# State-space groups: clipped distances move from VectorE to ScalarE one slab sooner, convolution goes ahead of mask and norm, softplus in four parts

## The reference, cut to what matters

```python
z, xbc, dt_raw, u_pool, gate_logits = jnp.split(h @ w_in, IN_SPLITS, axis=-1)
xbc = silu(causal_depthwise_conv(xbc, conv_w, conv_b))      # 4 taps
xs, bmat, cmat = jnp.split(xbc, ...)
dt = softplus(dt_raw + dt_bias);  a_cont = -exp(a_log)
a_cs = cumsum(dt * a_cont)
M[l, s] = (cmat[l] . bmat[s]) * exp(a_cs[l] - a_cs[s])      # for s <= l, else 0
y = M @ (xs * dt) + d_skip * xs                             # per head
y = rmsnorm(y * silu(z)) per group;  y_ssd = y @ w_branch_ssd
```

## Time and profile before

| | us |
|---|---|
| median of three runs | 1355.06 |
| lowest, highest | 1347.4, 1355.24 |
| the profiled execution | 1352.02 |
| its span, first to last instruction | 1350.1 |
| its mean granted TensorE clock | 0.966 of full |

### The profile page before, as it was taken

The page is one execution under the profiler, slowest core; times in us unless marked ns, Lnnn a source line. Parts: engine busy times, 40 slices in busy tenths (PEclk is TensorE's granted clock), DMA queues, the critical chain, the costliest instruction groups (busy, mean ns, idle before and its releaser), DMA issues.

```text
span 1350.1 us, 27191 instructions
## 1 busy us (share of the span) xinstructions
PE 1271.1 (94%) x9944; PEld 1235.0 (91%) x9944; DVE 957.2 (71%) x1728; ACT 698.0 (52%) x1077; POOL 28.8 (2%) x58
## 2 busy tenths in 40 slices
PE   6878899999999999999999989999999998999997
PEld 6867899999999999999999879899899997999997
DVE  4574578888788886778888888787876555555554
ACT  4325465555545445455555566666665334544442
POOL 0000000000000000000000000000000000000000
PEclk9889899999999999999999979999999998899998
DMA  6421356666467555856665525445336453455540
GB/s 262 125 63 63 134 179 205 207 210 222 168 234 261 194 208 223 266 169 208 217 215 179 182 91 192 141 155 171 124 126 199 159 187 125 142 186 186 182 160 31
DMA packets 71007, 234.66 MB, mean 174 GB/s; under 512 B 7056, under 2 KB 15376, under 8 KB 70304
## 3 DMA queue, kind: packets, MB, share of 16 engines
q1 hardware_dynamic: 63280, 203.87, 45.2%
q0 software_dynamic: 7664, 29.92, 6.7%
HBM read 232.69 MB, written 1.08 MB: 173 GB/s over the span
## 4 chain that ended last, share of the span: by engine, by line
PE 48%; DVE 31%; issue 10%; ACT 9%; DVEq 1%; DMA 0%; ACTq 0%; SPq 0%; PEldq 0%
PE ps L182 14%; PE ps L184 13%; PE ps L183 13%; DVE w_lo L174 13%; DVE arena L827 3%; ACT w_hi L169 3%; DVE arena L821 2%; DVE arena L829 2%; ACT arena L771 2%; PE ps L213 2%; DVE arena L1527 1%; DVE b_lo L850 1%; DVE arena L357 1%; ACT arena L565 1%; PE ps L1267 1%
## 5 line engine op out<-in xcount | busy, mean ns | idle before, releaser
L182 PE MATMUL ps<-a_hi,w_hi 128*128 128x256 f32 x1912 | 561.3, 294 | 9.4 <-DVE a_lo L1136 5.3
L174 DVE TENSOR_TENSOR w_lo<-w_raw,w_hi 128x1024 fp32r<-128x1024 f32 x381 | 462.1, 1220 | 142.8 <-ACT w_hi L169 140.5
L183 PE MATMUL ps<-a_lo,w_hi 128*128 128x256 f32 x1912 | 549.3, 287 | 0.0
L184 PE MATMUL ps<-a_hi,w_lo 128*128 128x256 f32 x1912 | 548.8, 287 | 0.0
L182 PEld LDWEIGHTS ps<-a_hi,w_hi 128*128 128x128 f32 x1912 | 375.1, 196 | 21.8 <-issue 14.8
L169 ACT ACTIVATE w_hi<-w_raw 128x1024 fp32r<-128x1024 f32 x381 | 386.7, 1046 | 13.9 <-DMA w_raw<-stream 7.2
L183 PEld LDWEIGHTS ps<-a_lo,w_hi 128*128 128x128 f32 x1912 | 375.8, 197 | 0.6 <-issue 0.2
L184 PEld LDWEIGHTS ps<-a_hi,w_lo 128*128 128x128 f32 x1912 | 375.4, 196 | 0.0
L182 PE MATMUL ps<-b_hi,w_hi 128*128 128x256 f32 x928 | 265.4, 286 | 8.0 <-DVE b_lo L850 4.1
L183 PE MATMUL ps<-b_lo,w_hi 128*128 128x256 f32 x928 | 262.5, 283 | 0.0
L184 PE MATMUL ps<-b_hi,w_lo 128*128 128x256 f32 x928 | 262.5, 283 | 0.0
(11 more groups left out here) (248 smaller groups left out, 1190.1 us busy)
## 6 DMA issues: line engine op xcount, KB each, us to landing
w_raw<-stream SPq DMA_DIRECT2D x381, 512.0 KB, 4.1
arena<-ada POOLq DMA_DIRECT2D x48, 512.0 KB, 5.5
c_hi<-cum_rows POOLq DMA_DIRECT2D x4, 1024.0 KB, 5.7
con<-consts SPq DMA_DIRECT2D x1, 1440.0 KB, 13.0
arena<-x SPq DMA_DIRECT2D x1, 1024.0 KB, 5.1
out<-arena SPq DMA_DIRECT2D x2, 512.0 KB, 3.0
arena<-c_rows POOLq DMA_DIRECT2D x1, 512.0 KB, 7.0
par<-params SPq DMA_DIRECT2D x1, 319.0 KB, 5.5
```

Of the source, the lines that this page charges most:

```text
L174: dve.tensor_tensor(w_lo[:, s % RING], w_raw[:, s % RING], w_hi[:, s % RING].bitcast(F32), ALU.subtract).then_inc(w_lo_ready, 1)
L182: pe.matmul(o, wh, xh, start=start, stop=False, skip_group_check=shared)
L183: pe.matmul(o, wh, xl, start=False, stop=False, skip_group_check=shared)
L184: return pe.matmul(o, wl, xh, start=False, stop=stop, skip_group_check=shared)
```

## The change

- `gaps` goes from VectorE to ScalarE. It is there a relu of cum[s] - cum[l] (bias a column of `cum_tok`, scale -1), and the exp takes scale -1. `neg_cum` becomes `cum_tok`, without its sign.
- ScalarE does relus and exps of two heads in slots 7 to 10 (`decays`), where the exps stood in 8 to 11, between `split_hi` and `used`. `decays(0)` waits for the spread cumulative sums and in group 0 for `own_copied`, `decays(2)` for the b_lo of the group before.
- VectorE, slot 5: convolution first, then the mask. The norm of the group before moves from slot 5 to slot 6, its b_lo behind x times dt in slot 7. ScalarE's copy into b_hi moves behind `split_hi` and silu(5) in slot 6. In the gates the norm moves from m = 5 to m = 6 too.
- The softplus is cut into four parts, behind the convolutions of slots 0 to 3 of group 0; `own` goes from slab 4 to slab 5, the copies of its result from slot 5 to slot 6, behind `split_lo`.
- In the gates the spread goes from m = 3 to m = 4.

```diff
@@ TensorE
-                    if j == 4 and not g:
+                    if j == 5 and not g:
                         own()
@@ gates
-                if m == 3:
+                if m == 4:
                     tail_spread(GROUPS - 1, None)
@@ ScalarE
+                def gaps(k):
+                    if k >= 4:
+                        act.wait_ge(y_done, in_group(k - 3, 8, g, it))
+                    for b in range(NB):
+                        c = slice(0, SEQ) if b == 0 else slice(SEQ, SEEN)
+                        ...
+                        act.activation(seen[k % 4][:, c], cum_all[:, k, b * P:SEQ], ACT.Relu, bias=cum_tok[:, b, h],
+                                       scale=-1.0).then_inc(gap_ready, 1)
+                def exps(k):
+                    act.wait_ge(gap_ready, in_group(2 * k + 2, 16, g, it))
+                    act.activation(seen[k % 4], seen[k % 4], ACT.Exp, scale=-1.0).then_inc(exp_done, 1)
+                def decays(k):
+                    if k == 0:
+                        act.wait_ge(cum_landed, in_group(16, 16, g, it))
+                    if k == 0 and not g:
+                        act.wait_ge(own_copied, 1)
+                    if k == 2 and g:
+                        act.wait_ge(yssd_ready, in_group(1, 1, g - 1, it))
+                    gaps(k)
+                    gaps(k + 1)
+                    exps(k)
+                    exps(k + 1)
                 for j in range(GRP):
-                    if g:
+                    if g and j != 6:
                         tail(j, g - 1, it)
                     split_hi(act, S_GRP + GRP * g + j + 3, it, GRP)
-                    if j >= 8:
-                        exps(2 * (j - 8))
-                        exps(2 * (j - 8) + 1)
                     if j == 6:
                         silu(5)
+                    if g and j == 6:
+                        tail(j, g - 1, it)
+                    if 7 <= j < 11:
+                        decays(2 * (j - 7))
                     used(j)
@@ VectorE
-                if j == 5:
+                if j == 6:
                     dve.wait_ge(inv_s_ready, in_group(1, 1, g, it))
...
                 for j in range(GRP):
-                    if g:
+                    if g and j != 7:
                         tail(j, g - 1, it)
-                    elif j in (0, 1):
-                        (softplus_series, softplus_and_cum)[j]()
                     split_lo(dve, S_GRP + GRP * g + j + 3, it, GRP)
-                    if j == 5:
-                        (wait for cb_ready, mask)
                     if j < 6:
                         ... (three taps)
+                    if j < 4 and not g:
+                        softplus_part(j)
+                    if j == 5:
+                        (wait for cb_ready, mask)
-                    if j == 5 and not g:
+                    if j == 6 and not g:
                         dve.wait_ge(own_ready, 1)
                         (copies of own)
                     if j == 7:
                         (x times dt)
+                    if g and j == 7:
+                        tail(j, g - 1, it)
                     if j >= 8:
                         (products of decay and mask)
-                    if 7 <= j < 11:
-                        gaps(2 * (j - 7))
-                        gaps(2 * (j - 7) + 1)
```

More of the change, by code:

```diff
@@ L1159, in build @@
         dt_f = area(SEQ)
-        dt_tok, neg_cum = area(NB, SSD_HEADS), area(NB, SSD_HEADS)
+        dt_tok, cum_tok = area(NB, SSD_HEADS), area(NB, SSD_HEADS)
         root_s = area(NB)
@@ L1369, in silu @@
                     act.activation(cv[:, j], cv[:, j], ACT.Silu).then_inc(act_done, 1)
-                def exps(j):
-                    act.wait_ge(gap_ready, in_group(2 * j + 2, 16, g, it))
-                    act.activation(seen[j % 4], seen[j % 4], ACT.Exp).then_inc(exp_done, 1)
+                def gaps(k):
[3 more added lines that the diff above has]
+                        c = slice(0, SEQ) if b == 0 else slice(SEQ, SEEN)
+                        h = GROUP_HEADS * g + k
+                        h = slice(h, h + 1) if it is None else bass.ds(it * GROUP_HEADS + h, 1)
+                        act.activation(seen[k % 4][:, c], cum_all[:, k, b * P:SEQ], ACT.Relu, bias=cum_tok[:, b, h],
[14 more added lines that the diff above has]
+                    exps(k + 1)
                 for j in range(GRP):
-                    if g:
+                    if g and j != 6:
                         tail(j, g - 1, it)
                     split_hi(act, S_GRP + GRP * g + j + 3, it, GRP)
-                    if j >= 8:
-                        exps(2 * (j - 8))
-                        exps(2 * (j - 8) + 1)
                     if j == 6:
                         silu(5)
+                    if g and j == 6:
+                        tail(j, g - 1, it)
+                    if 7 <= j < 11:
+                        decays(2 * (j - 7))
                     used(j)
@@ L1444, in ssd_vec @@
             dve.scalar_tensor_tensor(out=dt_e[h], in0=dt_x[h], scalar=-1.0, in1=dt_x[h], op0=ALU.mult, op1=ALU.max).then_inc(dt_x_ready, 1)
[L1446 to L1463, removed]
+            def softplus_part(n):
+                if n == 0:
+                    dve.wait_ge(dt_e_ready, 1)
+                    step(dve.tensor_scalar(dt_z[h], dt_e[h], 2.0, None, ALU.add))
+                    step(dve.reciprocal(dt_z[h], dt_z[h]))
+                    step(dve.tensor_tensor(dt_z[h], dt_z[h], dt_e[h], ALU.mult))
+                    step(dve.tensor_tensor(dt_e[h], dt_z[h], dt_z[h], ALU.mult))
+                if n == 1:
+                    step(dve.tensor_scalar(dt_f[h], dt_e[h], 1.0 / 15, None, ALU.mult))
+                    for d in range(13, 6, -2):
+                        step(dve.scalar_tensor_tensor(out=dt_f[h], in0=dt_f[h], scalar=1.0 / d, in1=dt_e[h], op0=ALU.add, op1=ALU.mult))
+                if n == 2:
+                    for d in range(5, 1, -2):
+                        step(dve.scalar_tensor_tensor(out=dt_f[h], in0=dt_f[h], scalar=1.0 / d, in1=dt_e[h], op0=ALU.add, op1=ALU.mult))
+                    step(dve.scalar_tensor_tensor(out=dt_f[h], in0=dt_f[h], scalar=1.0, in1=dt_z[h], op0=ALU.add, op1=ALU.mult))
+                    step(dve.tensor_scalar(dt_f[h], dt_f[h], 2.0, None, ALU.mult))
+                if n == 3:
+                    step(dve.scalar_tensor_tensor(out=dt_f[h], in0=dt_x[h], scalar=0.0, in1=dt_f[h], op0=ALU.max, op1=ALU.add))
+                    dve.wait_ge(decay_a, 1)
+                    step(dve.tensor_scalar(dt_x[h], dt_f[h], neg_a[h, 0:1], -1.0, ALU.mult, ALU.mult))
+                    step(dve.memset(dt_e[h], 1.0))
+                    dve.tensor_tensor_scan(cum[h, 0:SEQ], dt_e[h], dt_x[h], 0.0, ALU.mult, ALU.add).then_inc(dt_ready, 1)
@@ L1502, in heads_of @@
                     return slice(c, c + n) if it is None else bass.ds(it * GROUP_HEADS + GROUP_HEADS * g + c, n)
[L1504 to L1512, removed]
                 for j in range(GRP):
-                    if g:
+                    if g and j != 7:
                         tail(j, g - 1, it)
-                    elif j in (0, 1):
-                        (softplus_series, softplus_and_cum)[j]()
                     split_lo(dve, S_GRP + GRP * g + j + 3, it, GRP)
-                    if j == 5:
-                        dve.wait_ge(cb_ready, in_group(1, 1, g, it))
-                        dve.scalar_tensor_tensor(out=cb, in0=const("tri", SEEN), scalar=-1.0, in1=ps[:, 4, 0:SEEN],
-                                                 op0=ALU.is_gt, op1=ALU.mult).then_inc(cb_masked, 1)
                     if j < 6:
@@ L1531, in group @@
                         ins.then_inc(conv_done, 1)
-                    if j == 5 and not g:
+                    if j < 4 and not g:
+                        softplus_part(j)
+                    if j == 5:
+                        dve.wait_ge(cb_ready, in_group(1, 1, g, it))
+                        dve.scalar_tensor_tensor(out=cb, in0=const("tri", SEEN), scalar=-1.0, in1=ps[:, 4, 0:SEEN],
+                                                 op0=ALU.is_gt, op1=ALU.mult).then_inc(cb_masked, 1)
+                    if j == 6 and not g:
                         dve.wait_ge(own_ready, 1)
-                        step(dve.tensor_copy(dt_tok.rearrange("p b h -> p (b h)"), ps[:, 5, 0:64]))
-                        dve.tensor_scalar(neg_cum.rearrange("p b h -> p (b h)"), ps[:, 5, 64:128], -1.0, None, ALU.mult).then_inc(own_copied, 1)
+                        dve.tensor_copy(dt_tok.rearrange("p b h -> p (b h)"), ps[:, 5, 0:64])
+                        dve.tensor_copy(cum_tok.rearrange("p b h -> p (b h)"), ps[:, 5, 64:128]).then_inc(own_copied, 1)
                         dve.wait_ge(own_copied, 1)
@@ L1542, in group @@
                                               dt_tok[:, b, heads_of(0, GROUP_HEADS)].unsqueeze(2).broadcast_to((P, GROUP_HEADS, SSD_P)), ALU.mult).then_inc(x_tok_ready, 1)
-                        if g:
```

(3 more changed lines are left out.)

## The result

The changed kernel takes 1365.37 us (median of 7, 1360.88 to 1367.06) against 1352.28 for the kernel before (7 runs, 1347.4 to 1355.24): ratio 1.0098, 95% interval 1.0078 to 1.0118. That is 13 us slower, where 10.5 us were forecast (sum) and 1363 us named. The forecast's "about 0.6% slower" was taken against 1355.06, the median of three runs that was known then; against the 1352.28 of seven runs it is 0.98%. The profiled execution took 1365.37 us with a span of 1363.3, 13.2 over the span of before.

A forecast was written before the change was run, and what follows sets the result against it. TensorE, busy 94% of the span, was taken as the bound. Terms -0.9 + 4.5 + 3.6 + 1.5 + 1.8 = +10.5 us gave 1362.5 on 1352.0 or 1365.6 on 1355.06; forecast 1363, range 1349 to 1373.

The forecast's parts named there:

- VectorE up to the turn: Groups 1 to 3: the turn of the x slabs starts 2.04 us sooner, with 0.4 us of waiting left.
- ScalarE's chain to the first head: Groups 1 to 3: late w_hi(11) and w_lo(11) delay the products; TensorE stands 3.8 us; -0.9 us in all.
- Clock: Heads and slab 9 in groups 1 to 3 run at 1.2 GHz after the 3.8 us wait: +4.5 us.
- rival 3: Clock twice as dear: 3 us low time for 1.5 behind each long stand, landing 8.2; 1372; chance 0.14.
- Group 0: Own copies and broadcast landing come late before the first head: +3.6 us, plus +1.5 us of clock.
- Gates: Norm moved to slot 6 delays w_hi(9), w_lo(9) and the last c_lo before the pool product: +1.8 us.
- Rivals 1 and 2: Whole program: 1, turn and head gains arrive, -13, 1341, chance 0.08; 2, no more clock drops, about +2, 1355, chance 0.20.

The follow-up runs named there:

- best1: The changed kernel with products ahead of w_lo in slots 8 to 11, softplus as before and VectorE's gates norm at m = 5: 1342.05 us, ratio 0.9932.

## Why the prediction was right, point by point

**VectorE up to the turn: right.** A wait of 0.4 us was forecast, 0.26 measured.

**ScalarE's chain to the first head: right in each link.** The forecast had 3.8 us of idle, the profile has 3.81. The relu, which no row of before showed, was taken at 0.50 and 0.39 us; these are the rows of the changed kernel by shape (count, busy us, mean ns):

```profile
L1379 ACT ACTIVATE arena<-c_hi,arena 128x256 f32<-128x256 f32 x32 | 16.0, 499 | 4.4 <-DMA c_hi<-cum_rows 4.1
...
L1379 ACT ACTIVATE arena<-c_hi,arena 128x128 f32<-128x128 f32 x32 | 12.5, 389 | 0.0
```

The run with the products first shows that the named place in VectorE's queue decides, and the doubled relus that each microsecond ahead of w_hi(11) counts. The page ScalarE: Activation LUTs of the Trainium skill, section Rules for kernel authors, prefers VectorE for a relu. The four operations agree with it in these runs: 0.99 us on VectorE in the run with the order alone, 1.48 on ScalarE. What staying on VectorE would give I had put at 0.4 us a group. With the distances on VectorE and the exps in slot 8 the head waits 2.28 us and not 3.81, which is 1.5, but that run changes both; and with the turn late (relus alone) the head waits less with the relus on ScalarE, 0.35 us instead of 1.05. The place decides more than the engine.

**Clock: right, a little too small.** Four low stretches at 1.49 us were forecast. Heads and following slab took 6.62, 5.59 and 6.49 us, 2.36, 1.33 and 2.23 more than the 4.26 at the upper clock, 5.9 in all. Groups 1 to 3 together were forecast at -0.9 + 4.5 = +3.6 and measured +5.2; most of the difference is this term. In group 1 the value of rival 3, a clock twice as dear (3 us), is nearer than my 1.49, in group 3 it is as near. In group 0 the stretch from the first head to the group's end is 1.4 us longer, as forecast.

**Group 0: mechanism right, term too small.** Forecast +3.6 and +1.5, measured +7.2. The turn waits for `own_copied` and the relus for the broadcast, as named. ScalarE and POOL of the changed kernel:

```profile
813.58 0.55 POOL L1850 DMA_DIRECT2D c_hi<-cum_rows  x1 [1.50 <-DMA cum_rows<-arena]
...
822.35 1.50 ACT L1379 ACTIVATE arena<-c_hi,arena 128x256 f32<-128x256 f32 x4 [4.06 <-DMA c_hi<-cum_rows]
```

That is a landing 8.7 us after the request, where I had taken 7 out of 5.2 to 8.2 although the row of before for this very load said 8.2. The request is at 813.58 and not 812.1, of which 1.0 is the later start of the whole stretch. First head: 829.09, 5.8 after the same offset, the upper figure of the forecast (4.8) and 1 us more.

**Gates: right up to the pool product, wrong in the place and in the time.** +1.8 us up to the pool product was forecast and 1.79 found. VectorE's w_lo(9) follows the norm only after 2.07 us of waiting for w_hi, where it was 0.41:

```profile
1019.55 1.23 DVE L174 TENSOR_TENSOR w_lo<-w_raw,w_hi 128x1024 fp32r<-128x1024 f32 x1 [2.07 <-ACT w_hi L169]
```

But I said the pool product's own wait would grow to 3 us. It fell to 1.36, since TensorE was already held up 1.9 us earlier by a w_lo that came late through the same delay. My own terms would have given 1.8 + 1.1 + 1.8 = 4.7 us of standing; the trace has 1.9 + 1.4 us, and the rest is the low clock behind the first of them. And the forecast added the +1.8 to the program's time. It did not arrive there: before had 1.5 us of low clock behind the pool product, which the changed kernel spends ahead of it, and all that follows group 3 lasts 369.9 us instead of 370.0.

**What compensated.** The sum had 10.5 us against 13.1 between the medians and 13.2 between the spans. Term by term the profiles have 1.6 us more in groups 1 to 3, 2.1 more in group 0 and 1.9 less in the gates with all that follows; 1.0 us is the later start of the groups, ahead of the change. So part of the agreement is luck: two terms were too small, and one that the forecast counted did not come. Rivals 1 and 2 fell: the turn's gain arrived, and was not kept.

## What to carry to other kernels

Work that is moved ahead of an engine's wait delays everything that the engine does after the wait. Here the exps were ready 2.4 us before they were used, because w_hi and w_lo of a slab three ahead stood between; so move the consumer's place in its queue together with the producer's. A stall that is removed pays only if the next arrival on the same path is earlier too: write down the whole chain to it, with the time at which each queue gets free, and look for the instruction that has its inputs and does not start. Work cut into pieces and laid between others on a full engine makes its own result later by all that goes between. And a stretch that got longer is not yet time: follow it to the end of the program, since a later arrival can swallow a loss that stood behind the old one.

## What the runs showed of the hardware

TensorE's clock fell to 0.50 of full (1.2 GHz) behind every stand of 3.8 to 5.2 us in front of a first head, in all four runs that had them in groups 1 to 3, and behind the three stands of 2.28 us in the run with the order alone. Behind the turn's 2.3 us it fell twice of three times in before and three times of three with the relus alone; behind the 1.3 us of products first and best1 it never fell. A stand around 2.3 us can thus cost 1.5 us more or nothing, in the same kernel. Length alone does not decide: it fell behind the 1.97 us for w_lo in group 0 of before and the 1.9 us for w_lo in the gates (four runs of four), and not behind the 2.12 us of group 0's first head in the run with the gates as before. In front of the pool product it fell behind 1.8 us in three runs of four and never behind 1.4.

The broadcast of the cumulative sums in group 0, among the weight loads, landed 7.0 to 9.5 us after its request in the ten profiles; its median over the four groups was 5.4 to 6.1.
